# Turning the weighted values back in two attentions: plain transposes and an addition on VectorE instead of a folding matmul

## What is computed

```python
    # even layer, neighbourhood attention: 128 keys for each query
        sc = jnp.einsum('bwhd,bwlhd->bhwl', q_r, kg).astype(jnp.float32) * scale + bias.astype(jnp.float32)[None]
        a = jax.nn.softmax(sc, axis=-1).astype(v.dtype)
        return jnp.einsum('bhwl,bwlhd->bwhd', a, vg)
    # odd layer, latent attention
        sc = (jnp.einsum('bqhd,bkhd->bhqk', qn_i, kn)
              + jnp.einsum('bqhr,bkr->bhqk', qr_i, kr)).astype(jnp.float32) * scale
        a = jax.nn.softmax(sc, axis=-1).astype(v.dtype)
        return jnp.einsum('bhqk,bkhd->bqhd', a, v)
```

## Time and profile before

| | us |
|---|---|
| median of three executions (1905.99 to 1907.38) | 1907.15 |
| the profiled execution | 1906.77 |
| its span | 1905.0 |
| TensorE busy | 1842.9 (97%) |
| VectorE busy | 1339.1 (70%) |
| ScalarE busy | 800.9 (42%) |
| GpSimd busy | 858.5 (45%) |

### The profile page before, as it was taken

How to read it: one execution, slowest core, us unless ns; L and a number is a source line. 1 busy time by engine, 2 the same in 40 slices (tenths; PEclk the granted TensorE clock), 3 DMA queues, 4 the chain that set the end, 5 groups by cost and what they waited for, 6 DMA issues and landing times. The chain is left out here.

```text
span 1905.0 us, 27049 instructions
## 1 busy us (share of the span) xinstructions
PE 1842.9 (97%) x9736; PEld 1565.9 (82%) x9736; DVE 1339.1 (70%) x2021; ACT 800.9 (42%) x1581; POOL 858.5 (45%) x568
## 2 busy tenths in 40 slices
PE   6999999989999999998999999999999999999999
PEld 5888888868799888786888888887898998888887
DVE  5599999936688425621569966675777776788886
ACT  6211211211388432211245453432788787445432
POOL 2251341342488563365546241223788874354211
PEclk9999999999999999998999999999999999999999
DMA  5112452573387556555433343495546557657744
GB/s 202 45 45 103 159 157 67 172 241 108 119 276 245 183 192 222 193 181 176 163 124 120 127 145 101 159 359 170 161 144 203 184 187 295 236 177 278 267 143 139
DMA packets 160107, 331.93 MB, mean 174 GB/s; under 512 B 32690, under 2 KB 66226, under 8 KB 159987
## 3 DMA queue, kind: packets, MB, share of 16 engines
q1 hardware_dynamic: 159986, 330.36, 50.9%
HBM read 207.63 MB, written 122.68 MB: 173 GB/s over the span
## 5 line engine op out<-in xcount | busy, mean ns | idle before, releaser
L191 POOL TENSOR_TENSOR w_lo_part<-w_raw,w_hi_part 128x1024 fp32r<-128x1024 f32 x56 | 152.8, 2737 | 362.4 <-ACT w_hi_part L183 342.7
L605 DVE SCALAR_TENSOR_TENSOR ie_acc<-ie_u,ie_wconv,ie_acc 128x1551 f32<-128x1551 f32 x120 | 262.9, 2191 | 3.1
L3449 PE MATMUL og_ps<-w_hi_part,bl_ring 128*128 128x512 f32 x672 | 216.6, 393 | 1.0 <-DVE bl_ring L2982 1.0
L245 PE MATMUL ie_ps<-rows_hi,w_hi_part 128*128 128x512 f32 x384 | 151.1, 393 | 0.4 <-DVE ie_stage L619 0.4
L245 PE MATMUL ie_ps<-rows_lo,w_hi_part 128*128 128x512 f32 x384 | 149.7, 390 | 0.0
L245 PE MATMUL ie_ps<-rows_hi,w_lo_part 128*128 128x512 f32 x384 | 149.6, 389 | 0.0
L3449 PEld LDWEIGHTS og_ps<-w_hi_part,bl_ring 128*128 128x128 f32 x672 | 126.2, 188 | 26.8 <-DVE bl_ring L2982 1.1
L2870 DVE TENSOR_TENSOR mla_pt_lo<-mla_ps_t,mla_pt_hi 128x512 fp32r<-128x512 f32 x160 | 108.8, 686 | 33.0 <-ACT mla_pt_hi L2839 32.0
L3449 PE MATMUL og_ps<-w_lo_part,bl_ring 128*128 128x512 f32 x336 | 130.8, 389 | 0.0
L2863 DVE TENSOR_REDUCE mla_min<-mla_ps_s 128x1 f32<-128x1024 f32 (+1 forms) x96 | 99.9, 1042 | 29.5 <-PE mla_ps_s L2780 28.0
L2839 ACT CAST mla_pt_hi<-mla_ps_t 128x512 fp32r<-128x512 f32 x160 | 94.2, 590 | 60.7 <-PE mla_ps_t L2790 57.2
(11 more groups left out here) (361 smaller groups left out, 5242.3 us busy)
## 6 DMA issues: line engine op xcount, KB each, us to landing
w_raw<-wall SPq DMA_DIRECT2D x62, 512.0 KB, 4.7
w_hi_part<-weight_blocks SPq DMA_DIRECT2D x28, 512.0 KB, 4.6
w_lo_part<-weight_blocks SPq DMA_DIRECT2D x28, 512.0 KB, 5.9
weight_blocks<-w_hi_part SPq DMA_DIRECT2D x26, 512.0 KB, 6.3
w_raw_tiles<-wall SPq DMA_DIRECT2D x16, 512.0 KB, 5.5
odd_sums<-w_raw_tiles SPq DMA_DIRECT2D x8, 1024.0 KB, 4.3
w_raw<-odd_sums SPq DMA_DIRECT2D x16, 512.0 KB, 4.1
w_flat<-wall SPq DMA_DIRECT2D x16, 512.0 KB, 8.8
```

The source lines that it names most:

```text
L191: pool.tensor_tensor(g.W[1][:, pair % 2, off:off + QCOLS], g.raw[:, n % 2, :], g.W[0][:, pair % 2, off:off + QCOLS].bitcast(F32), ALU.subt ...
L245: mm = pe.matmul(psum[:, u % banks], w_at(g, name, a, k * HALF + c * P, P), g.XT[m][:, k, b * 512:(b + 1) * 512], start=i == 0, stop=i == ...
L605: dve.scalar_tensor_tensor(acc[:], ubuf[:, cc, s:s + CW], wconv[:, cc, s:s + 1], acc[:], ALU.mult, ALU.add).then_inc(taps, 1)
L3449: mm = pe.matmul(ps[:, N % 4], bl.part(a, N)[:, k], wb.at(N // HT, m, k), start=k + a + m == 0, stop=k == 3 and a == 1)
```

## The change

In both attentions the matmul with `fold` becomes two plain transposes with the identity, which deliver 128 columns for each tile: the high half and the low half beside each other. A new instruction on VectorE, a `tensor_reduce` over an innermost axis of two elements that lie 64 apart (`halves`), adds them within the same PSUM buffer (`added`), and a semaphore `joined` leads to the multiplication.

In `mla` the norm is split in two. `dve_join` (the addition and the reciprocal) stands in the even step at the end, behind `lo(step-2)`. `dve_norm` (the multiplication) stands in the odd step after it, behind that step's `minimum`. In `natten` addition and multiplication both stay where the norm was. The constant `fold` and its two loads go. The other stages keep their instructions and their order.

```diff
-def attention_tail(g, pl, ps_pv, ps_back, pv_sb, sums, rinv, fold, fold_in):
+def halves(ps_back):
+    return ps_back[:, 0:2 * P].rearrange("p (a t d) -> p a d t", a=2, t=2)
+
+def added(ps_back):
+    return ps_back[:, 2 * P:3 * P].rearrange("p (a d) -> p a d", a=2)
+
+def attention_tail(g, pl, ps_pv, ps_back, pv_sb, sums, rinv):
...
     def pe_back(pe, h6, q):
-        pe.wait_ge(fold_in, 16)
         pl.wait(pe, "copied", h6 + q + 1)
         pl.wait(pe, "normed", h6 + q)
         for a in range(2):
-            mm = pe.matmul(ps_back[:, a * DH:(a + 1) * DH], pv_sb[:, q % 2, a * P:(a + 1) * P], fold[:], start=True, stop=True)
-        mm.then_inc(pl["back"], 1)
-
-    def dve_invert(dve, h6, q):
+            tr = pe.transpose(ps_back[:, a * P:(a + 1) * P], pv_sb[:, q % 2, a * P:(a + 1) * P], g.ident[:])
+        tr.then_inc(pl["back"], 1)
+
+    def dve_join(dve, h6, q):
+        pl.wait(dve, "back", h6 + q + 1)
+        dve.tensor_reduce(added(ps_back), halves(ps_back), AX.X, ALU.add).then_inc(pl["joined"], 1)
         dve.reciprocal(rinv[:, q % 2], sums[:, q % NG]).then_inc(pl["inverted"], 1)
 
     def dve_norm(dve, h6, q, dst):
-        pl.wait(dve, "back", h6 + q + 1)
         pl.wait(dve, "inverted", h6 + q + 1)
-        dve.tensor_tensor(dst, ps_back[:, 0:P].rearrange("p (a d) -> p a d", a=2),
+        pl.wait(dve, "joined", h6 + q + 1)
+        dve.tensor_tensor(dst, added(ps_back),
...
# natten, VectorE
                 dve.reciprocal(rinv[:, u % 2], sums[:, u % NA_U]).then_inc(inverted, 1)
                 dve.wait_ge(back, u + 1)
+                dve.tensor_reduce(added(ps_back), halves(ps_back), AX.X, ALU.add).then_inc(joined, 1)
                 dve.wait_ge(inverted, u + 1)
+                dve.wait_ge(joined, u + 1)
...
# mla, VectorE
                 for step in steps:
                     if live(step):
                         minimum(h, step)
-                    if step % 2 == 0 and live(step - 8):
-                        q = (step - 8) // 2
+                    if step % 2 and live(step - 9):
+                        q = (step - 9) // 2
                         dst = out[:, 2 * (q % NG):2 * (q % NG) + 2, bass.ds(h * DH + q // NG * DH, DH)]
-                        dve_invert(dve, h * NG, q)
                         dve_norm(dve, h * NG, q, dst)
                     if live(step - 2):
                         lo(h, step - 2)
+                    if step % 2 == 0 and live(step - 8):
+                        dve_join(dve, h * NG, (step - 8) // 2)
```

More of the change, by code:

```diff
@@ L708 @@
     CREDITS = {"scored": 0, "minned": 2, "exped": 0, "turned": 3, "hi": 0, "lo": 2, "weighed": NG + 1,
-              "copied": 1, "back": 2, "inverted": 0, "normed": 1, "prepped": 1}
+              "copied": 1, "back": 2, "inverted": 0, "joined": 0, "normed": 1, "prepped": 1}
     def __init__(self, g, name, **credits):
@@ L851, in natten @@
         T = [even.T, sb("table", [P, 2, 3, 384])[:]]
-        fold = even.fold
         Q1 = [even.Q1, sb("q_hi", [P, TOK], F32R)[:]]
@@ L870, in natten @@
         QK_IN = 16 * 3
-        v_in, fold_in, attn_out = sem("v_in"), even.fold_in, [sem("attn_out0"), sem("attn_out1")]
+        v_in, attn_out = sem("v_in"), [sem("attn_out0"), sem("attn_out1")]
         tabled, vsplit = sem("tabled"), sem("vsplit")
@@ L875, in natten @@
         scored, minned, exped, turned = sem("scored"), sem("minned"), sem("exped"), sem("turned")
-        hi, lo, weighed, copied, back, inverted, normed = [sem(n) for n in ("hi", "lo", "weighed", "copied", "back", "inverted", "normed")]
+        hi, lo, weighed, copied, back, joined, inverted, normed = [
+            sem(n) for n in ("hi", "lo", "weighed", "copied", "back", "joined", "inverted", "normed")]
         NTILES, NPAIRS = HEADS * NA_T, HEADS * NA_U
@@ L1031, in turn_back @@
                 pe.wait_ge(copied, u + 1)
-                if u == 0:
-                    pe.wait_ge(fold_in, 16)
-                else:
+                if u >= 1:
                     pe.wait_ge(normed, u)
                 for a in range(2):
-                    mm = pe.matmul(ps_back[:, a * DH:(a + 1) * DH], pv_sb[:, u % 2, a * P:(a + 1) * P], fold[:], start=True, stop=True)
-                mm.then_inc(back, 1)
+                    tr = pe.transpose(ps_back[:, a * P:(a + 1) * P], pv_sb[:, u % 2, a * P:(a + 1) * P], g.ident[:])
+                tr.then_inc(back, 1)
             for u in range(NPAIRS + 4):
@@ L2721, in mla @@
         g.wait_attn = lambda eng, q: pl.wait(eng, "normed", (HEADS - 1) * NG + q)
-        act_copy, pe_back, dve_invert, dve_norm = attention_tail(g, pl, ps_pv, ps_back, pv_sb, sums, rinv, fold, fold_in)
+        act_copy, pe_back, dve_join, dve_norm = attention_tail(g, pl, ps_pv, ps_back, pv_sb, sums, rinv)
         nb = sum(ML_BATCHES)
@@ L3635, in lay_out @@
         "wall": np.stack([by[n] for n in WALL]),
[L3636 removed]
+        "c_ident": np.eye(P, dtype=np.float32),
         "g_pre_cols": cols(f["g_pre"][0]), "g_pre_row": f["g_pre"][1:2], "g_post": f["g_post"],
```

15 lines of the change are left out of this document (5 added, 10 removed).

## The result

| | before | after |
|---|---|---|
| median, us | 1907.48 (6 runs, 1905.99 to 1908.35) | 1913.59 (6 runs, 1912.79 to 1920.42) |
| profiled execution, us | 1906.77 | 1912.79 |
| its span, us | 1905.0 | 1911.2 |

The change makes the kernel slower. The ratio is 1.0045, with a 95% interval from 1.0034 to 1.0055; the medians alone give 1.0032, since some runs of the kernel after lie well above its median. The forecast was 1918.6 us, slower, with a range from 1907 to 1932.

A forecast was written before the change was run, and what follows sets the result against it. TensorE was taken to set the pace in both attentions, VectorE close behind in the neighbourhood one. +1.5 us (neighbourhood) and +9.9 (latent) made +11.4: 1906.8 becomes 1918.2, the median 0.4 above, 1918.6 us; range 1907 to 1932.

The forecast's parts named there:

- TensorE's two slots: Both attentions, TensorE: four weight-load slots a pair become two, saving 0.22 us a pair, 10.6 us in each attention.
- rival E: Both attentions: a transpose holds TensorE 0.275 us, so each pair loses 0.11 us; 1939.7 us, chance 0.02.
- The addition's price: VectorE, both attentions: the new addition of 256 elements takes 0.41 us, priced like the minima.
- C: VectorE, both attentions: the addition is cheap, 0.29 us; 1908.4 us, chance 0.11.
- D: VectorE, both attentions: the addition is dear, 0.68 us, for elements 64 apart; 1941.6 us, chance 0.05.
- The stall in the latent attention: TensorE's turning back waits for the multiplication, now behind the odd step's minimum: 20.5 us lost, net +9.9 us.
- the wait for GpSimd: Latent attention, before the last head: TensorE's existing 3.4 us wait takes up about 0.3 us of the loss.
- Rival B: Latent attention: the wait for the multiplication stays hidden and the 10.6 us gain is kept; 1898 us, chance 0.08.
- the 10.6 us: Neighbourhood attention: TensorE's saving from the shorter transposes, forecast to be lost because VectorE becomes the later engine.
- VectorE's round without waits: Neighbourhood attention: VectorE's instruction times without waits for others, summed over six rounds to 15.58 us a head.
- the addition with its wait: Neighbourhood attention, VectorE: addition 0.41 us plus 0.13 us wait for its result, 0.54 us a round.
- The 0.5 us at the end of the stage: Neighbourhood attention's end: turning back and multiplying alternate through one buffer; two links grow by 0.54 - 0.22 each.

The follow-up runs named there:

- e4_even: Against the changed kernel: in the latent attention addition, reciprocal and multiplication all stand in the even step behind the minimum, ahead of the low parts; 1902.31 us.
- e7_around_lo: Against the changed kernel: in the latent attention's even step, addition and reciprocal stand ahead of the low parts and the multiplication behind them; 1901.0 us.
- e2_mla_only: Against the kernel before: only the latent attention gets the change's edits, the neighbourhood attention keeps the folding product; 1916.5 us, ratio 1.0056.
- e8_na_late: Against e4_even: in the neighbourhood attention the multiplication moves behind the next round's first minimum; 1897.87 us.
- e6_even_end: Against the changed kernel: in the latent attention the multiplication moves into the even step, directly behind addition and reciprocal, which stay behind the low parts; 1905.42 us.

## Why the prediction was right, and where it was off

**TensorE's two slots: right in price, not in what they bring.** Rounds 0, 2 and 3 of `e4_even` fall by 0.22 to 0.26 us a pair. The premise that TensorE sets the pace in all of the latent attention was read from its busy time, and rounds 1, 4 and 5 refute it: there the low part was the limit, and with nothing stalled (`e7_around_lo`) rounds 4 and 5 still bring nothing. In the kernel after this hardly shows, because the stalls take up those waits. The reading that a record's 275 ns is mostly latency holds: records of 286 ns leave a gain, and rival E, by which the transposes would cost more than the folding passes, falls.

**The addition's price: right.** Forecast 0.41 us from the minima, measured 0.423 on average over 96 (0.409 to 0.433). So C (0.29) and D (0.68) fall by the price. By the time alone C would not have: 1913.6 us lies as near to C's 1908.4 as to the forecast of 1918.6. The distance of 64 between the summands costs nothing that shows.

**The stall in the latent attention: right in mechanism and sum, not in every round.** The stalls before `mla_ps_back` were forecast at 20.5 us and measure 18.6. The distances between pairs were forecast to grow by 10.2 us (9.9 in the prediction, which counts the gain for 48 pairs and not for the 47 distances) before the wait for GpSimd takes up its share, and grew by 8.9. By round, summed over all heads (the first two rows from start to start before `mla_ps_back`, less 0.11; the last two the distances between pairs, forecast by the prediction's own stalls less 0.22 a pair):

| us | round 0 | 1 | 2 | 3 | 4 | 5 | sum |
|---|---|---|---|---|---|---|---|
| stalls, forecast | 6.0 | 4.8 | 1.5 | 1.5 | 2.9 | 3.9 | 20.5 |
| stalls, measured | 6.8 | 4.5 | 1.2 | 1.2 | 2.6 | 2.3 | 18.6 |
| distances, forecast | +4.2 | +3.1 | -0.3 | -0.1 | +1.1 | +2.2 | +10.2 |
| distances, measured | +5.2 | +2.6 | +0.2 | -0.2 | +1.4 | -0.3 | +8.9 |

In rounds 1 to 4 the forecast was within 0.5 us over all heads. Round 0 costs 1.0 us more than forecast and round 5 costs 2.5 less, so the sum comes out nearer than the single rounds do, and that part is luck. The miss of round 5 has two causes. First, in three of the eight heads it has no stall at all and even becomes shorter (4.43 us). In these three ScalarE had no rounding of weights to do ahead of the high part, and in the other five it had one of 1.06 us. Kernel after, one of the five and one of the three:

```profile
1575.21 1.06 ACT L3070 CAST w_hi_part<-w_flat 128x1024 fp32r<-128x1024 f32 x1
1576.14 0.61 ACT L2846 CAST mla_pt_hi<-mla_ps_t 128x512 fp32r<-128x512 f32 x1
```

```profile
1502.74 0.59 ACT L2846 CAST mla_pt_hi<-mla_ps_t 128x512 fp32r<-128x512 f32 x1 [0.21 <-PE mla_ps_t L2797]
```

With the rounding, the high part starts 2.22 us after the `mla_ps_back` before it (1573.92 in the first of these), and ScalarE was not idle ahead of it; without, it starts after 1.63 us (1501.11 in the second) and has waited for TensorE. What hangs on it, down to the multiplication, then comes early enough. It is so in all eight heads, and the trace of the kernel before has the rounding in the same five. The prediction read one of these and took it for all eight. Second, the prediction took round 5 as having no wait of its own. In the kernel before, TensorE waits 0.14 us there before the weighing (0.17 where 0.03 is usual); with two slots less this would be 0.37, and the stall of round 4 uses it up. So in the five heads with a stall the round grows by 0.12 us and not by 0.27. Rival B, in which the wait stays hidden, falls: the idle time stands in the profile, and `e4_even` shows what that case would have been worth.

Of the stage's +7.4 the pairs make 8.9, and -1.5 lies ahead of the first pair. That part is scatter between executions: `e2_mla_only`, with the same edits, does not have it, and `e8_na_late` has it where `e4_even`, equal in this attention, does not.

**The neighbourhood attention: the mechanism right, one term mis-sized.** VectorE did become the later engine, and most of the 10.6 us was lost there: 2.3 us were gained where a loss of 1.5 was forecast. The step that failed is VectorE's round without waits. It counted the multiplication with its whole record, 0.29 us, while every other instruction was counted from start to start. The rows of after show 0.21 from the multiplication to the next minimum (571.43 to 571.64). Six times 0.07 to 0.08 is 0.4 to 0.5 us a head, where the whole head is 0.47 shorter than forecast (15.11 and not 15.58); over eight heads this is 3.8 us, the whole miss of this stage. Two smaller slips went the same way: in the two rounds of a head with 256-wide minima one of them was given 0.44 us, from a row that contained a short wait, and takes 0.36 (571.64 to 572.00), 0.2 us a head; the addition with its wait takes 0.1 us a head less. Against them stand 0.24 us a head of waits for the turned product before the addition, where the prediction had none. The 0.5 us at the end of the stage should by its own terms have been 0.6 (twice 0.54 - 0.22), which changes nothing.

**The sum.** Forecast +11.4 us on the profiled execution, measured +6.2 between spans. The difference of 5.2 is 3.8 in the neighbourhood attention, 1.0 in the pairs of the latent attention and 1.5 ahead of them, less 1.2 in the stage behind; the last two are scatter. So the direction and both mechanisms were right, and the size was about double what was measured, most of it by the one mis-sized term.

**What stays open.** Why round 0 takes 6.09 and 6.10 us in two heads and 5.64 to 5.78 in four, and which wait gives `e6_even_end` its longer rounds 0 and 2. That the chain from the transposes over the high and the low part to the weighing limits rounds 4 and 5 is read from the trace; no kernel shortened it.

## What to carry to other kernels

Before a consumer is moved a step later, list every single buffer that it frees, and who waits for that at the end of the same step: here one multiplication moved behind one minimum, with the addition behind the low parts, cost TensorE 18.6 us of stalls in 47 pairs, while the same move cost nothing in the attention where nobody waited for it early. An own-engine result is best consumed one instruction later, since a successor that waits for it starts 0.10 to 0.15 us behind its end instead of 0.08 before, but only where the freed buffer allows it. When an engine with 84% of its time busy gets 0.5 us a round more, add up its round in start-to-start distances throughout, since the one instruction a round counted by its record was worth 0.07 to 0.08 us, most of 3.8 us here. And before time saved on an engine is counted as gained, look for the waits that it has already, by distances between starts: 0.14 us in two of six rounds did not show in its busy time.

## What the runs showed of the hardware

- A VectorE multiplication of two SBUF operands stands still while GpSimd works on SBUF: 128 elements took up to 3.51 us instead of 0.28, ending 0.15 us behind GpSimd's instruction each time. With one operand in PSUM, none of 36 overlapping ones exceeded 0.293 us (`e7_around_lo`). I had expected the buffer in SBUF to be the better one.
- A busy TensorE is not always the one that sets the pace. The stretch before showed it busy for 210.00 of 210.00 us, and in three of six rounds two fewer weight loads a pair brought nothing, because the weighing waited for the low parts (shown by a kernel for round 1, by the rows for rounds 4 and 5).
- A pass with 64 columns cost TensorE the same 0.11 us as one with 128: four of the first kind became two of the second, and a pair took 0.22 us less wherever nothing else was the limit (rounds 2 and 3).
